# Head pairs in array halves, later sums of squares, and the norm factor on queries and keys, in a four-layer transformer kernel

## What is computed

```python
# layer 0: differential attention, 8 heads of two maps of width 64
s = q @ k.T * 64**-0.5 - slope * |qpos - kpos|   # two maps for each head
a = softmax(s[0]) - lam * softmax(s[1]);  o = rmsnorm(a @ v, subln) * 0.8
# layer 1: neighbourhood attention, 16 heads of width 64, bias on q, k and v
s = q * 64**-0.5 @ k.T + rpb_bias;  o = softmax(s) @ v
# both: h += o @ w_o;  h += (silu(n(h) @ w_gate) * (n(h) @ w_up)) @ w_down
#       h += sigmoid(n(h) @ ple_w_gate) * (p @ ple_w_proj)
# layer 2: convolution and poolings ("ev" weights), conv feed-forward
# layer 3: 8 heads with forget gates, 8 with a relative bias, causal; conv feed-forward
# n(x) = x * rsqrt(mean(x*x) + 1e-6) * gamma
```

## Time and profile before

| | |
|---|---|
| runs, median (lowest to highest) | 1371.92 us (1369.88 to 1372.73) |
| profiled execution, its own time | 1375.4 us |
| its span | 1373.6 us, mean granted clock 0.977 |
| busy: TensorE, VectorE, ScalarE, GpSimd | 1314.8, 942.8, 677.4, 163.7 us |
| chain that ended last | TensorE 82%, VectorE 9%, ScalarE 3%, DMA 2%, GpSimd 2% |
| read from HBM | 222 MB, 164 GB/s over the span |

### The profile page before, as it was taken

One profiled execution on the slowest core, in us unless ns is written; L12 is line 12 of the kernel. 1 busy time (PEld: TensorE's weight loads), 2 busy tenths in 40 slices (PEclk: granted clock), 3 DMA queues, 4 the chain that ended last, 5 costly groups with the idle time before them and its releaser, 6 DMA issues.

```text
span 1373.6 us, 22269 instructions
## 1 busy us (share of the span) xinstructions
PE 1314.8 (96%) x8682; PEld 1183.8 (86%) x8682; DVE 942.8 (69%) x1215; ACT 677.4 (49%) x975; POOL 163.7 (12%) x157
## 2 busy tenths in 40 slices
PE   5999889999989999999998999999999999999996
PEld 4988778888978778888888999999888888999985
DVE  4777669775675666777657687887658555777753
ACT  4456536544545545555445335555445455555541
POOL 3001351001120002000012611300011000100001
PEclk8999999999999999999999899999999999999998
DMA  7424497655544235766564456865555423666550
GB/s 269 154 95 121 117 227 210 188 169 192 189 141 153 93 93 141 194 186 182 172 204 154 143 188 177 248 188 176 176 177 166 139 90 97 165 182 183 176 183 31
DMA packets 286134, 224.22 MB, mean 163 GB/s; under 512 B 8216, under 2 KB 276544, under 8 KB 285936
## 3 DMA queue, kind: packets, MB, share of 16 engines
q1 hardware_dynamic: 283888, 214.25, 51.6%
q0 software_dynamic: 2176, 8.99, 2.3%
HBM read 222.15 MB, written 2.63 MB: 164 GB/s over the span
## 4 chain that ended last, share of the span: by engine, by line
PE 82%; DVE 9%; ACT 3%; DMA 2%; POOL 2%; issue 1%; SPq 0%; POOLq 0%; DVEq 0%; ACTq 0%
PE ps L1540 21%; PE ps L1531 12%; PE ps L1532 11%; PE ps L1533 11%; PE ps L1541 10%; PE ps L1728 3%; DVE wlo L985 3%; PE ps L1774 2%; PE ps L1539 2%; DMA raw<-in_ffn_w_up 1%; PE ps L1748 1%; DVE x L1011 1%; PE ps L1647 1%; PE ps L1648 1%; PE ps L1649 1%; ACT whi L643 1%
## 5 line engine op out<-in xcount | busy, mean ns | idle before, releaser
L985 DVE TENSOR_TENSOR wlo<-raw,whi 128x2048 fp32r<-128x2048 f32 (+1 forms) x206 | 470.1, 2284 | 156.7 <-ACT whi L643 155.7
L643 ACT CAST whi<-raw 128x2048 fp32r<-128x2048 f32 (+1 forms) x206 | 385.4, 1873 | 262.7 <-PE ps L1533 145.2
L1531 PE MATMUL ps<-x,whi 128*128 128x256 f32 (+1 forms) x1640 | 478.2, 292 | 10.5 <-DVE x L1011 6.2
L1532 PE MATMUL ps<-x,whi 128*128 128x256 f32 (+1 forms) x1640 | 466.9, 285 | 0.0
L1533 PE MATMUL ps<-x,wlo 128*128 128x256 f32 (+1 forms) x1640 | 466.8, 285 | 0.0
L1531 PEld LDWEIGHTS ps<-x,whi 128*128 128x128 f32 (+1 forms) x1640 | 316.8, 193 | 25.8 <-issue 13.0
L1532 PEld LDWEIGHTS ps<-x,whi 128*128 128x128 f32 (+1 forms) x1640 | 316.9, 193 | 0.5
L1533 PEld LDWEIGHTS ps<-x,wlo 128*128 128x128 f32 (+1 forms) x1640 | 316.9, 193 | 0.0
L1540 PE MATMUL ps<-hid,whi 128*128 128x512 f32 x672 | 236.7, 395 | 0.0
L1540 PE MATMUL ps<-x,whi 128*128 128x512 f32 x616 | 225.7, 405 | 4.5 <-DVE wlo L985 4.5
L1541 PE MATMUL ps<-hid,wlo 128*128 128x256 f32 x672 | 188.4, 280 | 0.0
(11 more groups left out here) (177 smaller groups left out, 1353.5 us busy)
## 6 DMA issues: line engine op xcount, KB each, us to landing
raw<-in_ffn_w_in SPq DMA_DIRECT2D x88, 512.0 KB, 5.1
raw<-in_ffn_w_gate SPq DMA_DIRECT2D x44, 512.0 KB, 4.0
raw<-in_ffn_w_up SPq DMA_DIRECT2D x44, 512.0 KB, 5.2
raw<-in_ffn_w_down SPq DMA_DIRECT2D x32, 512.0 KB, 4.0
raw<-in_ffn_w_out SPq DMA_DIRECT2D x32, 512.0 KB, 4.4
raw<-in_da_w_qkv SPq DMA_DIRECT2D x24, 512.0 KB, 4.8
raw<-in_na_w_qkv SPq DMA_DIRECT2D x24, 512.0 KB, 4.4
raw<-in_od_w_in SPq DMA_DIRECT2D x24, 512.0 KB, 4.6
```

Of the source, the lines that this page charges most:

```text
L643: nc.scalar.copy(whi[:, c % RING, 0:n], raw[:, c % RING, 0:n]).then_inc(w_hi, 1)
L985: nc.vector.tensor_tensor(wlo[:, c % RING, 0:n], raw[:, c % RING, 0:n], whi[:, c % RING, 0:n].bitcast(F32), ALU.subtract).then_inc(w_lo, 1)
L1531: mm(dst, hi, x[:, 0, :], start=start, stop=False)
L1532: mm(dst, hi, x[:, 1, :], start=False, stop=False)
```

## The change

1. `sum_squares` moves to ahead of the third chunk in `t_op`, to the middle of the second chunk in `ffn`; `spread_r` to ahead of the fourth chunk and to the middle of the third. For `mix2` a new `f_pair` runs tiles 0 to 5 of the first two chunks before tiles 6 and 7 of both. The last quarter of x is loaded ahead of the third chunk at the start.
2. The scaled second input goes (`scaled`, `scaled_hi`, `scaled_lo`). Queries and keys are computed from x, and `take_qk` on VectorE multiplies them by r as they leave PSUM; in layer 1 `qk_bias` on ScalarE adds the bias afterwards. The forget gates get the same multiplication (`f_raw`).
3. The attention's unit of work is a pair j of heads over two steps: `scores(j)` issues both heads, alternating the halves of 64 rows; `times_v(j)` in layers 1 and 3 alternates the halves of 64 columns. The orders of all queues are rewritten.
4. The bias masks on GpSimd wait until the up-projection is done (`w_used`, `START["down0"]`, `START["down2"]`). In layer 0 the transposed output moves from bank 6 to the upper half of bank 7.

```diff
-O_BUF, N_BUF = 0, 1
+O_BUF, N_BUF = (1, 0, 1), (0, 1, 0)
-SUM_AFTER, SPREAD_AT = 0, (2, 0)
+SUM_AT = {"v0": (2, 0), "v1": (2, 0), "v3": (2, 0)}
+SPREAD_AT = {"v0": (3, 0), "v1": (3, 0), "v3": (3, 0)}
...
             load_x(2)
+            load_x(3)
             load_chunk("v0", 2)
-            load_x(3)
...
+                    gp.wait_ge(w_used, START["down0"])
...
+            gp.wait_ge(w_used, START["down2"])
...
+            def qk_bias(i):
+                ac.wait_ge(qk_raw, i + 1)
+                for f in range(2):
+                    to = qk_tile(i) + f
+                    ins = nc.scalar.activation(qkT[:, to, :], qkT[:, to, :], ACT.Identity,
+                                               bias=pcol(COL_BQK + to))
+                ins.then_inc(copied, 1)
...
+                    j = (s - 4) // 2
+                    if s % 2 == 0:
+                        if a == 1 and 2 <= s <= 16:
+                            qk_bias(s // 2 - 1)
+                        if a == 0 and s >= 8:
+                            take_o(j - 2)
+                        if a and 0 <= j - 1 < PAIRS:
+                            take_T(2 * j - 1)
+                        if 0 <= j < PAIRS:
+                            exps(2 * j)
+                            exps(2 * j + 1)
+                        if a and 0 <= j - 1 < PAIRS:
+                            take_o(j - 1)
+                        if a == 0 and 0 <= j - 1 < PAIRS:
+                            take_T(j - 1)
+                            square_o(j - 1)
+                        if a and 0 <= j < PAIRS:
+                            take_T(2 * j)
                         if s < STEPS - 3:
                             split(START[qk] + s // 2 + RING)
...
+            def take_qk(name, i):
+                ve.wait_ge(w_used, START[name] + i + 1)
+                src = bank(QK_BANKS[i % 3]).rearrange("p (f t) -> p f t", f=2)
+                dst = qkT[:, qk_tile(i):qk_tile(i) + 2, :]
+                if i % 2 == 0:
+                    ins = nc.vector.scalar_tensor_tensor(out=dst, in0=src, scalar=0.125,
+                                                         in1=over2(rst[:]), op0=ALU.mult,
+                                                         op1=ALU.mult)
+                else:
+                    ins = nc.vector.tensor_tensor(dst, src, over2(rst[:]), ALU.mult)
+                ins.then_inc(qk_raw if name == "qk1" else copied, 1)
...
+                split(c + RING)
+                split(c + 1 + RING)
                 means(mix)
-                split(c + RING)
                 diagonals(mix)
-                take_r(mix)
-                scaled(a, 0)
-                scaled(a, 1)
-                scaled_lo(a, 0)
-                split(c + 1 + RING)
...
                 split(c + 2 + RING)
                 take_v(a)
+                take_r(mix)
                 split(c + 3 + RING)
...
+                    if s % 2 == 0:
+                        if 2 <= s <= 16:
+                            take_qk(qk, s // 2 - 1)
+                        if 0 <= j < PAIRS:
+                            bias_max(2 * j)
+                            bias_max(2 * j + 1)
+                        if a == 0 and s >= 8:
+                            lo_out(j - 2)
+                        continue
+                    if a == 0 and 0 <= j - 1 < PAIRS:
+                        norm_o(j - 1)
+                    if a and 0 <= j - 1 < PAIRS:
+                        lo_out(j - 1)
+                    if 0 <= j < PAIRS:
+                        normalise(2 * j)
+                        if a == 0:
+                            normalise(2 * j + 1)
+                    if 3 <= s < STEPS - 1:
                         split(START[qk] + s // 2 - 1 + RING)
+                    if a and 0 <= j < PAIRS:
+                        normalise(2 * j + 1)
...
-                    middle = (lambda: spread_r(name)) if first and jj == 1 else None
+                    middle = None
+                    if first and jj:
+                        middle = lambda: (sum_squares if jj == 1 else spread_r)(name)
...
+                def scores(j):
+                    if j % 2 == 0:
+                        pe.wait_ge(copied, COPY_BASE[qk] + j + 2)
+                    if j:
+                        pe.wait_ge(sc_free, base + 2 * j)
+                    forget = a == 2 and j < 4
                     for t in range(TT):
                         off, n = span(a, t)
                         ts = slice(t * P, (t + 1) * P)
+                        for m in range(2):
+                            rows = slice(DH * m, DH * (m + 1))
+                            ins = mm(bank(4 + m)[:, off:off + n], qkT[rows, j, ts],
+                                     qkT[rows, 8 + j, 0:n], start=True, stop=not forget)
+                            if t == 1 and not forget:
+                                ins.then_inc(sc_out, 1)
...
+                        for kt in range(TT):
+                            q0 = P if a == 2 and kt == 1 else 0
+                            for m in range(2):
+                                u, rows = 2 * j + m, slice(DH * m, DH * (m + 1))
+                                pt = probT[:, m, :]
+                                ins = mm(b[rows, q0:S], v[:, kt, u * DH:(u + 1) * DH],
+                                         pt[:, tcol(a, kt, q0 // P):tcol(a, kt, 1) + P],
+                                         start=(kt == 0), stop=(kt == TT - 1))
...
                 def halfway(s):
+                    j = (s - 4) // 2
+                    if s % 2 == 0 and 0 <= j < PAIRS and (a or j % 2 == 0):
+                        scores(j)
                     if a == 0:
                         if s % 2 == 0 and s >= 8:
-                            o_transposes((s - 8) // 2)
-                        if s % 2 == 1 and 7 <= s < 23:
-                            times_v((s - 7) // 2)
+                            o_transposes(j - 2)
+                        if s % 2 == 1 and 0 <= j - 1 < PAIRS:
+                            times_v(j - 1)
+                    elif s % 2 == 1 and 0 <= j < PAIRS:
+                        transposes(2 * j)
+                    elif s % 2 == 0 and 0 <= j - 1 < PAIRS:
+                        transposes(2 * j - 1)
...
+            f_pair(EV_BANKS[0:2], START["ev"], "mix2")
+            sum_squares("mix2")
+            for i in range(2, COUNT["ev"]):
```

More of the change, by code:

```diff
@@ L100 @@
      "final"))}
-XBUF = {"mix0": 0, "ffn0": 1, "ple0": 1, "mix1": 0, "ffn1": 1, "ple1": 1, "mix2": 0, "ffn2": 0,
-        "mix3": 0, "ffn3": 1, "final": 1}
+XBUF = {"mix0": 0, "ffn0": 0, "ple0": 0, "mix1": 1, "ffn1": 1, "ple1": 1, "mix2": 0, "ffn2": 0,
+        "mix3": 0, "ffn3": 0, "final": 1}
 def sums_of(n):
@@ L887, in _ @@
             take_x("mix0", 2)
+            take_x("mix0", 3)
             squares("mix0", 0)
@@ L899, in _ @@
                 wo, gate = f"wo{layer}", f"gate{layer}"
-                for i in range(2):
-                    split(START[f"v{layer}"] + i + RING)
-                scaled_hi(layer)
-                for i in range(2, 4):
-                    split(START[f"v{layer}"] + i + RING)
+                splits(f"v{layer}")
                 attention(layer)
@@ L920, in _ @@
                         split(START[gate] + i + RING)
-                    pair(target, i)
+                        pair(target, i)
+                take_x(target, 3)
+                squares(target, 3)
                 split(last(gate) + RING)
@@ L947, in _ @@
             down(2, "mix3")
-            for i in range(2):
-                split(START["v3"] + i + RING)
-            scaled_hi(2)
-            for i in range(2, 4):
-                split(START["v3"] + i + RING)
+            splits("v3")
             cf = START["f3"]
-            ac.wait_ge(w_used, cf + 1)
-            link(nc.scalar.activation(osb_f(prob)[0], bank(F3_BANK)[:, 0:S], ACT.Abs,
-                                      bias=pcol(COL_BF)))
+            ac.wait_ge(f_raw, 1)
+            fz = prob[:, 0, S:2 * S]
+            link(nc.scalar.activation(osb_f(prob)[0], fz, ACT.Abs, bias=pcol(COL_BF)))
             link(nc.scalar.activation(osb_f(prob)[0], osb_f(prob)[0], ACT.Exp, scale=-1.0))
@@ L1575, in f_chunk, with f_pair @@
                 ins.then_inc(w_used, 1)
+            def f_pair(banks, c, name):
+                x = xs[XBUF[name]]
+                for k0, k1 in ((0, 6), (6, KT)):
+                    for i in range(2):
+                        hi, lo = slot8(whi, c + i), slot8(wlo, c + i)
+                        pe.wait_ge(w_lo, c + i + 1)
+                        for k in range(k0, k1):
+                            x_ready(name, k)
+                            for f in range(2):
+                                cs = slice(f * P, (f + 1) * P)
+                                ins = three(bank(banks[i])[:, f * S:(f + 1) * S], hi[:, k, cs],
+                                            lo[:, k, cs], x[:, k, :, :], k == 0 and f == 0,
```

(7 more changed lines are left out.)

207 lines of the change are left out of this document (51 added, 156 removed).

## The result

The changed kernel took **1375.47 us** (median of 7 runs, 1374.16 to 1380.29), the kernel before 1370.67 beside it (7 runs, 1369.88 to 1372.73): a ratio of **1.004, 95% interval 1.0025 to 1.0055**. I had said 1356.8, faster with a chance of 0.80. It is slightly slower; the time is inside the range I gave, but the direction was wrong.

What follows compares the result with a forecast made beforehand. TensorE, busy 96% of the span, was taken as the bound, with queue order deciding in the attentions. Norms -24.3 and attention +9.2 gave -15.1: 1360.3 us, less 3.5 for the median, 1356.8; range 1334 to 1378.

Steps and rivals of the forecast that it cites:

- Layer 0: Its attention: in-order queue loop, odd turns 12.7 us, even 13.9 (+1.2 for held scores); +18, +3 for slow-clock turns: +21.
- The norms: Sums of squares issued later in mixers and feed-forward blocks, removing TensorE's waits for GpSimd's additions: -24.3 us over all eight.
- ffn1, ffn3: Feed-forward blocks: 2.2 us of wait and 3.3 of clock saved each, 1.7 and 0.9 given back: -4.0 and -4.7.
- mix0: First mixer: sum after two chunks at 23.4, 2 us idle remaining: -7.5, or -4 if the clock falls again.
- mix1: Layer 1's mixer: chunk 1 fills 4.85 us of idle, 3.0 of clock go, 1.7 come back: -6.
- mix2, ffn2 and mix3: Stretch to layer 3's first scores: mix2 -3.2 (VectorE's chain starts 3 us earlier), ffn2 +0.6, mix3 -0.5.
- ffn0: First feed-forward block: short wait saved, 1.7 us back at chunk 3, chunk 6's load issued 3 us later: +1.
- Two heads in halves: Scores, and values in layers 1 and 3: a pair's eight matmuls overlap in 1.27 us; ends 1.05 and 1.9.
- The rival of the halves that take turns: Pair matmuls in the attentions run serially, 1.9 us: total change -3.7, 1368 us; chance 0.20 shared with moved waits.
- the rival in which each change of half drains: In the attentions each change of half drains TensorE, 0.2 us: +13 in all, 1385 us; chance 0.15.
- Layers 1 and 3: Their attentions: pairs of 10.3 and 9.3 us, pairs with forget matmuls in layer 3 losing 1.2 each: -4.4 and -7.4.
- the waits of the norms only moved: Rival at the norms (chunk 3, mix0 at low clock): norms -12, 1369 us; chance 0.20 shared with halves taking turns.

Runs made afterwards that it cites:

- ffn_sums_late_alone: The kernel before, with only the feed-forward sums of squares moved to mid chunk 1 and the spread to mid chunk 2: 1373.52 us, ratio 1.0007.
- heads_serial: The changed kernel with all matmuls of a pair's head 0 ahead of head 1's, not alternating, outside the forget heads' scores: 1378.43 us, ratio 1.005.
- best_orders: The changed kernel with layer 0's queues reordered, ScalarE's output copy before second-head exponentials in layers 1 and 3, feed-forward spread ahead of chunk 2: 1331.5 us, ratio 0.971.

## Why the prediction was wrong

By the traces, layer 0 came out 6.3 us worse than its term, the norms 10.3 worse, layer 1 1.0 worse and layer 3 4.0 better: +13.6 on a forecast of -15.1.

**Layer 0, +27.3 for +21: the mechanism was right, its size off.** The odd turns are 12.7, 12.6 and 12.1 us where the working said 12.7, and VectorE idles 4.2 to 5.1 us a turn for GpSimd's norm, as the text named. The "+1.2" of an even turn is the 1.22 us seen above, and its 13.9 is 14.0 at full clock, by the estimate above; with the low clock the first two took 15.0 and 16.0, of which "+3" for slow scores was a fair guess. What failed is the third even turn, 18.4 us and not 13.9. It holds the start of the output product, ahead of which TensorE waits for the last copy, 5.35 us in the first profile:

```profile
PE ps L1501 <- DVE qkT L1075: 5.4, 1, 5.4
```

I had counted that wait for layers 1 and 3 and left it out for layer 0, where the loop makes it longest. With the fall of the clock around it (0.73 in that turn) it is 4.5 of the 6.3 us missed. Another 1.5 is the turn behind the sixth, 9.3 us where it had been 7.8, which my sum left out.

**The norms, -14.0 for -24.3** (the rows of the table outside the attentions). This is the larger miss. The step that failed: a term took the whole wait for GpSimd as saved and gave back only what the later factor and a late split cost where I had looked. That the chunk or the scores right behind the wait were not ready either, I had put at nothing.
- ffn1, ffn3: the text has "2.2 us of wait and 3.3 of clock" and gives back only chunk 3's 1.7 and 0.9, which came (1.39 and 0.58). But chunk 1's split ends 1.8 us after TensorE asks for it; it had been hidden under the sum's wait. -2.0 and -2.5 for -4.0 and -4.7, and what is left is the clock, not the wait. ffn_sums_late_alone says it most plainly: 2.3 us of wait turned into 3.1.
- mix0: "I put the sum at 23.4"; it came at 25.5, after 3.35 us of idle for the 2 that I allowed. A GpSimd addition took 2.85 us, for 1.57 before, and VectorE's means stand behind two splits until 29.5. The clock fell again, for 6.8 us, which was the upper end of that term (-4): -4.4 for -7.5.
- mix1: the wait for the sum is gone, and 1.87 us for a split stand in its place, for which I had 1.7. What I had at nothing is 1.42 us ahead of the first scores, for the bias on queries and keys. The text says of the new passes on them that their amounts "cost nothing" and prices their place in the queues only inside the attentions. -4.3 for -6.
- mix2, ffn2 and mix3, +2.3 for -3.1: mix2 itself is not the miss. By the same matmuls in both traces TensorE gains 8.1 us up to the end of the second chunk, gives back 3.1 at the factor and a split, and 3.1 more where it waits for VectorE's convolution, 2.46 us for 0.79 before, with 3.4 us at half clock behind it: -1.8 for -3.2. VectorE's chain did come 3 us earlier. ffn2's chunks lost 0.7 for 0.6. What the sum had at nothing is 1.2 us at the end of ffn2's up-projection, where GpSimd's masks slow VectorE (last section), and 3.4 us ahead of layer 3's first scores: 1.43 us of wait for a split and 1.64 for VectorE's copy of queries and keys, both behind the forget gates' copies in VectorE's queue.
- ffn0 was too dark (-3.1 for +1): the late chunk 6 cost less, 2.79 us of wait against 4.46 before, and behind it the clock stayed up, where it had been at half for 6.8 us.

**Two heads in halves.** 1.07 us for a pair, where I took 1.27 with 1.05 as the end: I was right that they overlap, but they do so fully. The Trainium skill, TensorEngine Tiling (Array Packing), Key Properties, says that tiles work independently; the eight matmuls in 1.07 us agree, in either order of the heads. The rival of the halves that take turns (1.9 us) and the rival in which each change of half drains are both refuted by these 1.07 us, and the second once more by heads_serial, which has one change of half where the changed kernel has many, and takes the same time.

**Layers 1 and 3.** Layer 1 came out as worked (-3.4 for -4.4), by the wait foreseen: 0.86 us a pair for the normalisation behind ScalarE's output copy (best_orders takes it away). The waits for copy and bias were longer than I had, 1.42 us three times and 2.85 once for 0.85 and 2.4, and my own terms, eight pairs of -1.09 with these four waits, add up to -3.8 rather than -4.4. Layer 3 gained 4 us more: its pairs with forget matmuls went from 12.5 us (two steps of 6.25) to 10.6, and the others from 10.34 to 9.1, where I had 9.3 and had the former lose 1.2 each. The forget matmuls are of full width and don't overlap, but the four score matmuls between them do, 0.42 and 0.63 us for both heads where one took that much before.

**From the traces to the medians.** The two profiled executions differ by 1.2 us (1375.4 and 1374.16), the medians by 4.8 the other way. The kernel before was profiled in an execution 4.7 us over its median of 1370.67 (I had 1371.92 for it), the changed one 1.3 under its own. I had seen 3.5 of this and taken it off. So the 18.7 us between forecast and median are 13.9 of miss between the executions (1360.3 and 1374.16), of which the table shows 13.6, the 3.5, and the 1.3.

**The range and the chances.** Nothing that I listed came alone. Layer 0's loop was near its upper bound and the waits of the norms only moved, and I had treated the second as a rival to the forecast and the first as a term in it. Together with my attentions of layers 1 and 3 (-11.8) they make +27 - 12 - 12 = +3. The 0.05 for "same" and 0.15 for "slower", by drains alone, were too low for a sum whose two largest terms stood against each other with errors of 6 and 10 us.

## What to carry to other kernels

When two units of work become one step, redo the order of every in-order queue in that step: draw the loop from an operation round to itself through all engines, and put work with slack (a weight split) where the engine would stand, and what the bottleneck engine waits for (a copy out of PSUM) ahead of what it does not. Here that was worth 50 us on the same instructions, from a ratio of 1.0044 to 0.9676. And before a wait is counted as saved, ask what the instruction behind it waits for: work hidden under a wait comes out with its full length when the wait goes.

## What the hardware showed beyond that

**Halves need adjacency, not alternation.** Head 0's matmuls all ahead of head 1's, each half still runs its own beside the other (1.07 us for both); one full-width matmul between them, and they follow one another (2.54 us).

**GpSimd's additions and VectorE's lengthen one another.** Ahead of ffn1's sum in the changed kernel:

```profile
540.03 0.80 POOL L505 TENSOR_TENSOR ssum<-ssum,sq 128x256 f32<-128x256 f32 x1
540.91 2.66 POOL L507 TENSOR_TENSOR ssum<-ssum,sq 128x256 f32<-128x256 f32 x1
...
540.15 5.56 DVE L962 TENSOR_TENSOR wlo<-raw,whi 128x2048 fp32r<-128x2048 f32 x2
```

The same addition takes 0.73 us ahead of ffn2's sum, where no split runs beside it, and 2.66 here; two splits take 5.56, where the two of ffn2 take 4.49. The change itself also moved additions: GpSimd's eight mask additions of ffn2, at 870 us before, now start at 971.87, while VectorE makes the last hidden tiles. One of VectorE's additions before, and the same one after, with the masks beside it:

```profile
966.91 0.42 DVE L1275 TENSOR_TENSOR acc<-acc,gu 128x256 f32<-128x256 f32 x1
```
```profile
971.87 10.98 POOL L612 TENSOR_TENSOR t5b<-t5b,cst 128x384 f32<-128x384 f32 x8 [102.95 <-PE ps L1503]
977.27 1.24 DVE L1243 TENSOR_TENSOR acc<-acc,gu 128x256 f32<-128x256 f32 x1
```

TensorE then waits 1.06 us for a hidden tile, a wait that the kernel before does not have and for which my forecast had "nothing, 2 us at worst". VectorE's pass at 971.75, which reads one input from PSUM, kept its 0.69 us beside the masks. The Trainium skill, SBUF — State Buffer, Who interferes with whom, says that a VectorE instruction with two inputs in SBUF contends with a GpSimd instruction that reads SBUF. The rows agree. They were read from the traces: no run here moved the masks or the sums alone.

**A busy TensorE kept its clock.** With the dummy matmuls the first four turns of layer 0 ran at 1.00, where without them they had 0.77, 1.00, 0.68 and 0.99. What that bought, the dummies took back by standing in the queue.
